# A hybrid decoder step on one core: cache pages spread further ahead, window values turned, selected blocks issued by GpSimd and ScalarE

## The reference, cut to what matters

```python
# differential attention, 8 heads, two maps per head (decode rows: over 4096 cached keys)
s = einsum('bqhcd,bkhcd->bhcqk', q, k);  p = masked_softmax(s, kpos <= qpos)
a = p[:, :, 0] - lam * p[:, :, 1];       o_d = einsum('bhqk,bkhv->bqhv', a, v)
# native sparse attention, 8 query heads over 2 KV heads, three branches
o_cmp  = attend(q, compress(cache))                  # blocks of 32 tokens, stride 16, through a small MLP
idx    = top_k(importance(p_cmp), 16)                # 16 blocks of 64 keys, 3 of them fixed
o_sel  = attend(q, selected blocks of cache_nsa_sel_kv)
o_win  = attend(q, last 512 keys: state_nsa_win_kv)  # the "window", or local, branch
o = concat(sum(branches * gates) * silu(z_n), rms_norm(o_d) * silu(z_d)) @ w_out + x
```

## Time and profile before

| | |
|---|---|
| median of 3 runs | 852.11 us (849.56 to 857.02) |
| profiled execution | 850.98 us, its span 849.2 us |
| granted TensorE clock, mean | 0.946 |
| busy: PE, DVE, ACT, POOL | 773.3, 450.8, 188.5, 109.1 us |
| HBM read, written | 213.77 MB, 10.04 MB |

### The profile page before, as it was taken

One profiled execution on the slowest core, in us unless ns is written; L12 is line 12 of the kernel. 1 busy time (PEld: TensorE's weight loads), 2 busy tenths in 40 slices (PEclk: granted clock), 3 DMA queues, 4 the chain that ended last, 5 costly groups with the idle time before them and its releaser, 6 DMA issues.

```text
span 849.2 us, 14846 instructions
## 1 busy us (share of the span) xinstructions
PE 773.3 (91%) x4891; PEld 376.9 (44%) x4891; DVE 450.8 (53%) x980; ACT 188.5 (22%) x484; POOL 109.1 (13%) x206
## 2 busy tenths in 40 slices
PE   6999999899989988999999998789889987887997
PEld 2465535354434535345534663234434333344443
DVE  2132242526404348796554746684885873684923
ACT  0411020002101102222132322432443441344000
POOL 0000000000000100020002026410264643000000
PEclk9999999999999979999999997989998977988999
DMA  9986796969896889978776149997799996772011
GB/s 339 305 284 206 267 326 235 380 228 373 275 368 204 296 317 355 371 266 288 277 264 206 36 143 336 356 304 264 262 297 302 339 315 223 232 327 124 1 50 52
DMA packets 128936, 220.67 MB, mean 260 GB/s; under 512 B 17481, under 2 KB 55282, under 8 KB 127514
## 3 DMA queue, kind: packets, MB, share of 16 engines
q1 hardware_dynamic: 109626, 194.32, 66.3%
q0 software_dynamic: 7712, 14.90, 5.4%
q10 hardware_dynamic: 11520, 10.49, 3.8%
HBM read 213.77 MB, written 10.04 MB: 264 GB/s over the span
## 4 chain that ended last, share of the span: by engine, by line
PE 61%; issue 12%; DMA 9%; DVE 9%; SPq 6%; POOLq 2%; POOL 1%; ACT 1%; DVEq 0%
PE banks L605 14%; PE banks L583 14%; PE banks L1027 7%; SPq L387 5%; PE banks L619 4%; PE banks L551 4%; DMA proj<-in_cmp_cache 3%; DMA ring<-in_dk_cache 3%; PE banks L840 2%; DMA ring<-in_dv_cache 2%; DVE att L1692 2%; PE banks L564 2%; POOLq L401 1%; PE banks L870 1%; PE banks L635 1%
## 5 line engine op out<-in xcount | busy, mean ns | idle before, releaser
L605 PE MATMUL banks<-ring,xt 128*128 128x512 f32 (+1 forms) x448 | 188.9, 575 | 0.0
L605 PEld LDWEIGHTS banks<-ring,xt 128*128 128x128 f32 x448 | 84.2, 193 | 93.9 <-issue 90.9
L583 PE MATMUL banks<-proj,wide 128*64 128x256 f32 x896 | 101.9, 389 | 1.6 <-DMA proj<-in_cmp_cache 1.6
L1251 ACT ACTIVATE wide<-banks,att 128x128 f32<-128x128 f32 (+3 forms) x128 | 66.3, 523 | 162.6 <-DVE att L1692 162.6
L405 POOL DMA_DIRECT2D ring<-in_sel_cache x156 | 82.3, 528 | 58.8 <-issue 52.5
L840 PE MATMUL banks<-ring,small 128*32 128x512 f32 x512 | 75.8, 671 | 10.7 <-DMA ring<-in_dv_cache 7.7
L583 PEld LDWEIGHTS banks<-proj,wide 128*64 128x64 f32 x896 | 65.1, 141 | 40.6 <-DMA proj<-in_cmp_cache 6.9
L619 PE MATMUL banks<-ring,small 128*32 128x512 f32 x512 | 66.1, 628 | 16.3 <-DMA ring<-in_dk_cache 16.3
L1417 DVE TENSOR_SCALAR small<-small 128x510 f32<-128x510 f32 x8 | 3.4, 426 | 142.4 <-ACT small L1096 127.6
L1081 ACT ACTIVATE proj<-banks,x_rs 128x512 f32<-128x512 f32 (+1 forms) x32 | 21.2, 663 | 199.6 <-PE banks L605 162.1
L886 PE MATMUL banks<-consts,wide 128*128 128x128 f32 x240 | 44.0, 309 | 18.5 <-DVE xt L1716 10.5
(11 more groups left out here) (344 smaller groups left out, 863.5 us busy)
## 6 DMA issues: line engine op xcount, KB each, us to landing
ring<-in_dk_cache SPq DMA_DIRECT2D x256, 256.0 KB, 6.0
ring<-in_dv_cache SPq DMA_DIRECT2D x256, 256.0 KB, 4.7
proj<-in_cmp_cache SPq DMA_DIRECT2D x144, 128.0 KB, 3.8
ring<-in_w_in SPq DMA_DIRECT2D x6, 2048.0 KB, 11.1
proj<-in_cmp_cache ACTq DMA_DIRECT2D x80, 128.0 KB, 5.5
ring<-in_sel_cache POOLq DMA_DIRECT2D x156, 32.0 KB, 5.1
ring<-in_x_nat SPq DMA_DIRECT2D x2, 2048.0 KB
ring<-in_cmp_cache SPq DMA_DIRECT2D x32, 128.0 KB, 4.1
```

Source lines behind the costliest of these rows:

```text
L583: last = mm(to, w1[:, kv, half, lp, :], rows[:, kv, g, lp, :, :, :], start=lp + half == 0, stop=lp == LP - 1 and half == 1, tile_position= ...
L605: last = mm(banks[:, 3 + n % 2, 0:width(c)], xt[:, k, P * t:P * t + P], w_ring[:, c % 2, k, 0:width(c)], start=k == 0, stop=k == KC - 1)
L1251: last = A(e_slot(j, c)[:, 0:n], banks[:, 2 * (j % 2) + c, 0:n], ACT.Exp, bias=row_max[:, j % 4, c:c + 1], accum_out=row_sum[:, j % 4, c:c ...
```

## The change

1. `K_LATE` becomes 3 for every tile: the K steps end in tile 9 of stage 2 (before: tile 11).
2. The softmax over the 4096 scores and the turn of its weights move up to tiles 10 and 11, and V steps 0 to 12 go beside tiles 11 to 15. One more stands behind the loop, the other 50 in rounds 0 to 58 (`v_round`), so that every sixth of these rounds has none. `pick` moves with them.
3. The window values swap operands: 32 matmuls with 32 columns of weights as the stationary operand and 128 value columns as the moving one, in four column groups of the array, a copy by VectorE, and two transposes (`win_values`, `win_turn`).
4. SyncE issues no selected block. Input weights 7 are loaded after the last K step. Of the first half ScalarE issues 42 in tiles 12 to 15, GpSimd 70. Of the second half GpSimd issues 86 and ScalarE 26, two in each of rounds 30 to 42.
5. Scratch moves (`probs_t`, `e_slot`, `v_masked`), and the prompt's compressed scores use banks 5 and 6.

The diff, cut to its core:

```diff
-        K_STEPS, K_TURN, K_LATE = 64, 6, (3, 2, 2)
-        V_EARLY = 4
+        K_STEPS, K_TURN, K_LATE = 64, 6, 3
+        V_EARLY, V_ROUNDS = 14, 60
@@
+        def v_round(v):
+            return (v - V_EARLY) * V_ROUNDS // (K_STEPS - V_EARLY)
+        def pick_round(b):
+            return v_round(8 * b + 8) if b < DEC - 1 else V_ROUNDS
@@
+        def sel_run(eng, kind, n, end, done="sel_in"):
+            while n < end:
+                q, slot = n // N_TOP, SEL_FIRST + n % N_TOP
+                to = min(end - n, N_TOP - n % N_TOP, 4)
+                sel_ranked(eng, kind, q, slot, slot + to, done)
+                n += to
@@ SyncE
-                if n == 49:
+                if n == 52:
                     ...
                     load_w(6)
-                if n == 58:
-                    sp.wait_ge(s("proj_ready"), 24)
-                    sp.wait_ge(s("new_proj_ready"), 6)
-                    load_w(7)
                 load_k(n)
+            sp.wait_ge(s("proj_ready"), 24)
+            sp.wait_ge(s("new_proj_ready"), 6)
+            load_w(7)
@@
             for v in range(64):
-                if v == 4:
-                    sp.wait_ge(s("proj_ready"), 28)
-                    sp.wait_ge(s("new_proj_ready"), 7)
-                    for b in range(2):
-                        sel_fixed(sp, mybir.EngineType.SP, b)
-                    for q in range(4):
-                        sel_load(q)
                 ...
                 load_v(v)
@@ TensorE
+            def win_values():
+                ...
+                for bh in range(2):
+                    for kt in range(4):
+                        for i in range(4):
+                            last = mm(banks[32 * i:32 * i + 32, 2, 256 + P * bh:256 + P * bh + P], p_win_t[:, kt, 32 * bh:32 * bh + 32],
+                                      win_v[:, 4 * bh + i, kt, :], start=kt == 0, stop=kt == 3, tile_position=(0, 32 * i))
+                last.then_inc(s("win_tensor"), 1)
@@
                 if i == 11:
+                    pe.wait_ge(s("scores_kept"), 8)
+                    pe.wait_ge(s("diff_weights"), 1)
+                    for g in range(PAGES):
                         ...
+                    pe.wait_ge(s("probs_kept"), 4)
+                    for v in range(2):
+                        v_step(v)
                 if i == 12:
+                    for v in range(2, 5):
+                        v_step(v)
@@ i == 13: v_step 5 to 7; i == 14: pick(0), v_step 8 and 9; i == 15: win_values, v_step 10 to 12
+            v_step(V_EARLY - 1)
+            win_turn()
@@ rounds
-                if j + V_EARLY < 64:
-                    v_step(j + V_EARLY)
+                for v in range(V_EARLY, 64):
+                    if j == v_round(v):
+                        v_step(v)
@@ ScalarE
+                if i == 10:
+                    act.wait_ge(s("diff_max"), 1)
+                    A(scores, scores, ACT.Exp, bias=work[:, 144:145], accum_out=work[:, 145:146]).then_inc(s("diff_exps"), 1)
@@ i == 12, behind the exponential c_exp
+                    for b in range(2):
+                        sel_fixed(act, mybir.EngineType.Activation, b)
+                    sel_run(act, mybir.EngineType.Activation, 0, 6)
                 if i == 13:
                     for k in range(4):
                         keep_turn(f"z{k}")
                     ...
+                    sel_run(act, mybir.EngineType.Activation, 6, 16)
@@ i == 14: sel_run(act, ..., 16, 26); i == 15: sel_run(act, ..., 26, 38)
@@ rounds
+                if 30 <= j < 43:
+                    sel_run(act, mybir.EngineType.Activation, 182 + 2 * (j - 30), 184 + 2 * (j - 30))
@@ GpSimd
-                for q in range(4 + 4 * n, 8 + 8 * n):
-                    sel_ranked(pool, mybir.EngineType.Pool, q, SEL_FIRST, 6, "sel_pool_in")
-                    ...
+                sel_run(pool, mybir.EngineType.Pool, *((38, 104), (104, 182))[n], "sel_pool_in")
```

More of the change, by code:

```diff
@@ L351, in late_k @@
         def late_k(i):
-            before = K_TURN * 6 + sum(K_LATE[n % 3] for n in range(min(i, 12)))
-            return range(before, before + (K_LATE[i % 3] if i < 12 else 0))
+            before = K_TURN * 6 + K_LATE * i
+            return range(before, min(before + K_LATE, K_STEPS))
+        def v_round(v):
+            return (v - V_EARLY) * V_ROUNDS // (K_STEPS - V_EARLY)
+        def pick_round(b):
+            return v_round(8 * b + 8) if b < DEC - 1 else V_ROUNDS
         def duo(j):
@@ L804, in _ @@
                         turn_blocks(f"z{k}")
+                    for v in range(5, 8):
+                        v_step(v)
                 if i == 14:
@@ L915, in values @@
                 last.then_inc(s("pv_n"), 1)
-            def pick(b):
-                pe.wait_ge(s("v_masked"), b + 1)
-                for m in range(4):
-                    last = mm(banks[:, 7, m:m + 1], v_masked[:, m // 2, P * (m % 2):P * (m % 2) + P], ones[:, 0:1],
-                              start=True, stop=True)
-                last.then_inc(s("v_picked"), 1)
             def sel_scores(n):
@@ L988, in _ @@
                     turn(j - 2)
-                if j < DUOS and j % 8 == V_EARLY:
-                    pick(j // 8)
-                if j + V_EARLY < 64:
-                    v_step(j + V_EARLY)
+                for b in range(1, DEC):
+                    if j == pick_round(b):
+                        pick(b)
+                for v in range(V_EARLY, 64):
+                    if j == v_round(v):
+                        v_step(v)
                 for n in range(2):
@@ L1603, in _ @@
             silu_z(25)
+            keep_scores(7)
+            dve.wait_ge(s("scores_kept"), 8)
+            V.tensor_reduce(work[:, 144:145], scores, AX.X, ALU.max, negate=True).then_inc(s("diff_max"), 1)
             dve.wait_ge(s("p_kc_roots"), 1)
```

223 lines of the change are left out of this document (115 added, 108 removed).

## The result

The changed kernel takes 869.95 us (median of 4 runs, 869.06 to 876.09) beside 850.84 us of the kernel before (847.71 to 857.02, 4 runs): ratio 1.0224, interval 1.0182 to 1.0266. The forecast was 854 us, the range 836 to 866. A median in this document is over all executions of a kernel; the ratios and the table of means leave out executions more than 1.5% above the fastest of the same kernel (one each of e1, e2 and e9, where it took 4179.64 us, and a few of the kernel before).

The account below looks back on a forecast made before the run. Stage 2 was taken as bound by TensorE's own work, the rounds by TensorE with VectorE close behind. 850.98 - 19.3 gained + 21.6 lost = 853.3 us, 854 against the median; range 836 to 866.

Parts of the forecast that it names:

- Clock: ... I count nothing for it: Half-clock rows behind the new 7.1 us wait, 2 to 3 us, taken as offset by a vanishing wait: counted nothing.
- z2: Tile 12: ScalarE's ten issues delay its copy, so TensorE waits 7.1 us instead of 0.39: 6.8 us lost (5 to 8).
- round 51: TensorE's 4.99 us wait before the selected scores and 1.5 us of slow rows end: 6.5 us gained.
- V pages: Rounds: pages come from 450 us instead of 500, so TensorE's waits for them go: 6 us gained (4 to 7.7).
- K steps: Stage 2, three per tile: TensorE waits for pages in tiles 16 to 19: 2 us lost (0 to 7).
- softmax: Tile 10: TensorE asks for the weights after 16.5 us, the chain takes 18.2: 1.7 us lost (0 to 4).
- round 19: GpSimd's 70 first-half blocks instead of 56 land late for `sel_place`: a new wait of 3.4 us (0 to 8).
- rounds 30 to 42: ScalarE's two issues and a load per round exceed its estimated 1.7 us slack: 3 us lost (0 to 6).
- late exponential: Start of the rounds: ScalarE's last twelve issues end after its first exponential is due: 2 us lost.
- B: Rival: pages bind stage 2, 865 us, chance 0.12; its sign is K waits over 10 us in tiles 16 to 25.
- Window values: Before the rounds: wide matmuls of 1.99 us and transposes of 0.3 us replace 9.18 us: 6.8 us gained.
- Rival A: ScalarE's issues stay hidden in tile 12 and the rounds, so their losses go: 841 us, chance 0.33.

Follow-up runs that it names:

- e1: The changed kernel with ScalarE's ten block issues of tile 12 moved ahead of the wait for the centred scores: 863.87 us, 1.0162 of the kernel before.
- e2: The changed kernel with V steps 8 to 11 in tile 14 and 12 and 13 behind tile 31: 866.85 us, 1.0162 of the kernel before.
- e9: e6 with the K steps of tiles 16 to 25 dealt out unevenly, two to four per tile: 848.99 us, 0.9946 of the kernel before.
- e4: The changed kernel with ScalarE's ten issues moved ahead, V steps spread out and window scores ahead of the turned weights: 854.37 us, 1.0008 of the kernel before.
- e10: The kernel before with the window values turned (wide matmuls, two transposes) as the only edit: 855.46 us, 1.002 of the kernel before.
- e8: The kernel before with three K steps per tile as the only edit: 857.82 us, 1.0072 of the kernel before.
- e11: The kernel before with its first ten block issues on ScalarE in tile 12, instead of SyncE, as the only edit: 860.46 us, 1.0096 of the kernel before.
- e7: The changed kernel without ScalarE's 26 issues in rounds 30 to 42, GpSimd issuing all 104 ranked second-half blocks: 878.19 us, 1.0317 of the kernel before.
- e12: e9 with twelve early V steps instead of fourteen: 840.97 us, 0.9868 of the kernel before.
- e5: The changed kernel with only ScalarE's last twelve issues moved, two in each of rounds 2 to 7: 872.48 us, 1.023 of the kernel before.
- e6: e4 with ScalarE's last twelve issues also moved, two in each of rounds 2 to 7: 847.24 us, 0.9975 of the kernel before.

## Why the prediction was wrong, step by step

**The step that failed is "Clock: ... I count nothing for it".** I had set one wait (z2, 2 to 3 us of slow rows) against one other (round 51) and called it even. That was wrong on paper already: the 1.5 us of slow rows behind round 51's wait stand in the 6.5 us of its gain, and I used them a second time here. In the runs the change has four long waits of TensorE that the kernel before had not (2.24, 6.89, 5.23 and 3.49 us), and time at 1.2 GHz rose by 36 us, which weigh 18: about the whole of the 16 us between forecast and result. Behind round 19, where the wait of round 51 went, it fell by 10 us; ahead of round 19 it rose by 48 by the profiled executions. Taking all four away (e4) gave 34 of the 36 us back, though a new wait of 9.28 us stands there. The rule that the prediction cites (the Trainium skill, TensorE: Matmul & The Clock Gate, "HAM oscillation") names this price; the traces agree in direction. They give no equal price per wait: behind 2.24 us it was 6.6 us in one run and none in another.

The rest of the sum came out nearly even (span x clock 802 for 801, forecast + 2.3 us), and part of that is luck. V pages, K steps and softmax cost 11 us more than forecast; round 19, rounds 30 to 42 and the late exponential, hidden here behind the waits for pages, cost 8 less.

**V pages: forecast - 6, measured + 1.6 us of waiting.** I saw that pages come from 450 us on, and not that V steps 10 to 13 stand in one burst just ahead of the rounds. A ring of four slots lets SyncE issue step n only when n - 4 is used, so the first rounds wait 5.23 and 3.49 us. Before there were four V steps in a row too, but then came 9.18 us of window values, in which the next pages could land. The saved matmuls had been cover for a transfer; I had costed them as a gain alone. e10 bears this out: with these matmuls short and all else as before, the first waits for V pages come in rounds 1 and 2 (1.36 and 1.34 us), in the kernel before only in round 3. e2 took the waits away by spreading the V steps.

**Late first exponential: forecast 2, measured 9.3 to 10.0 us** once the pages were in time (e2, e4). I priced twelve issues at 0.54 us and three loads at 0.87; they took from 531.7 to 544.8, 13.1 us, with the DMA engines full. A price taken from a quiet stretch was used in a full one.

**K steps: forecast 2 (0 to 7), measured 4.9** in waits (7.5 us in tiles 16 to 25, before 2.6), 6 alone (e8). The place and the mechanism were right, the size was too small. B's sign, over 10 us of K waits in tiles 16 to 25, was not met: 4.0 of the 11.5 us above lie ahead of tile 16, and behind tile 20 there is one wait of 0.83 us.

**Softmax in tile 10: forecast 1.7, measured 2.24**, and 6.6 of slow rows behind it, which was in no term.

**z2: forecast 6.8, measured 6.5** (6.89 for 0.39), 7.07 in e11. Right, and so was the price of the ten issues: they run from 493.01 to 502.13 us, 9.1 us for 9.2. The page that the prediction cites calls the time to start a DMA "usually small relative to the DMA itself" (the Trainium skill, DMA: Bandwidth & Descriptors, "Issuing engines are not separate DMA queues"). One issue is small here too, 0.49 us against a median of 4.8 until its data has landed; but ten in a row hold ScalarE's copies, and in e11 they alone cost 8 us.

**Window values: forecast - 6.8, measured - 6.8 in its own rows** (1.96 + 0.44 for 9.18), but alone it gained nothing (e10): my arrangement had a wait behind it.

**Round 51: forecast - 6.5; e7 puts the wait back and loses 8.** Right. **Rounds 30 to 42: forecast 3, measured 0** (e7). The issues found room in those rounds, so my 1.7 us of slack was too low; a mean waiting time is no bound.

**Round 19: forecast 3.4, measured 0.** GpSimd's last ranked block was issued by 596.5 us, 61.6 us after the first round (forecast 64.5), but the rounds had become so slow that round 19 came at 614.5, 79.6 us after it (forecast 65.5). GpSimd's time was nearly right, TensorE's was not, and that the wait stayed away is luck.

**V steps that cover less: forecast 2.7.** No run tells it apart; it stays open.

Rival A (841 us, issues hidden) is e12's time, but not a forecast that came true: A was about the change as written, and there z2 stood for 6.89 us. e12 has issues, V steps and K steps in other places.

What stays open: why the clock fell behind some waits of about 2 us and not behind others, why it fell in the kernel before with no wait ahead of it (e10), and where e12's gain over e9 comes from. No wait of chosen length was tried in a place of choice.

## What to carry to other kernels

When a change adds waits to TensorE, list every one, and give each a second price: the rows behind it at half clock (here from nothing in e2 to 8.2 us in e5, behind the same wait of 2.24 us). When it takes work away from TensorE, ask which transfer that work had covered. After the first wait is taken away look for the one under it: an edit that is worth nothing alone (e5) may be worth something after another (e6: 3 us by the ratios, whose intervals overlap, 7 by the medians). And span x 2 x (1 - mean clock) over all executions says in one line whether lost time is work and waits or clock.

## What the runs showed of the hardware that was not expected

- The mean granted clock of the changed kernel lies below that of the kernel before in every execution: 0.915 to 0.925 in its four, 0.931 to 0.948 in the 26 of the kernel before (0.942 to 0.955 in the six of e12).
- The clock can fall with TensorE never idle: from 1.00 to 0.50 during and behind the window values of the kernel before (503 to 518 us).
- An issue by ScalarE takes 0.49 us at the median, but a load of block numbers 0.28 to 2.96 us, and twelve blocks with their loads 1.09 us each while the DMA engines are full (DMA share 1.00 to 1.07 from 535 to 545 us).
- Moving 2 of 14 V steps into the rounds brought 6.6 us by the ratios (e9 to e12, 0.9946 to 0.9868), though TensorE waits no less for pages (3.8 and 4.5 us); e12's clock is 0.948 to e9's 0.939, and the cause is open.
